# Second attention of a two-block kernel: probabilities divided before the transposes, values as the stationary operand, RMS factors applied to the two halves of the output projection

## The chip, the cores and the metric

The kernel runs on one core of a Trainium2 chip. The metric is the device time of one execution in microseconds (us), as the median over several executions.

## The reference

Two transformer blocks follow each other on 256 tokens of width 1024. The change lies in the second one. After its projections it has 8 query heads of kind A (windowed, two key/value heads, with one more "sink" score per head in the softmax denominator) and 8 heads of kind B (neighbourhood attention with a bias), all of width 64. Every query sees 256 latent keys and 256 context keys. Then each kind's 512 outputs are normalised by their own root mean square, and both go through one output projection:

```python
p = jax.nn.softmax(jnp.concatenate([s_loc, s_ctx, sink_col], axis=-1), axis=-1)      # kind A; kind B has no sink
o = einsum('bnkgqj,bnjkd->bnqkgd', p_loc, vb) + einsum('bnkgqj,bjkd->bnqkgd', p_ctx, v_ctx)
...
jnp.concatenate([_rms_norm(o_a, g_a), _rms_norm(o_b, g_b)], axis=-1) @ w_out
...
x = x + g1 * merged; x = x + g2 * swiglu(modulate(rms_norm(x)))
```

All is float32.

## The kernel before, in words

The program is one instruction stream per engine, written out by hand in its order; semaphores join them. The second attention works on 32 tiles (`tiles2`): token block b (128 queries) of 2, kind (0 is A, 1 is B), head h of 8. A tile has 128 queries by 512 keys. Tiles go in pairs p = 0 to 15: pairs 0 to 3 and 8 to 11 are kind A, the others kind B. "Pair A" and "pair B" below mean a pair of that kind.

- **TensorE.** For each p: `scores2(p)` (L985; 64-row products, the two tiles side by side in the array, and for the mask or bias full 128x128 ones), then `turn2` of both tiles of pair p-1 (L994; four 128x128 transposes each, of the exponentials E2), then `values2` of both tiles of pair p-2 (L1010; per tile four products with the transposed exponentials, 128x128, as the stationary operand and 64 columns of V moving). A float32 product is two records of the profile, a transpose one.
- **VectorE** takes each tile's row maximum (L2050 and, with the sink, L2051 for A; L2054 for B). After eight tiles it copies their outputs from PSUM (L2013, `outputs`); the division by the sums for eight heads of both kinds is done once per token block (L2025 to L2032, `divide`).
- **ScalarE** in iteration n takes the exponential of tile n (L1484, with the row sum as a second, small instruction) and then copies the transposed tile n-2 from PSUM (L1491). `sink_exp` (L1469) and the squares of the outputs (L1476) come once per token block.
- **Buffers.** E2 and PT2 (the transposed tiles) have four places each, the scores four PSUM banks, the transposes two, the outputs the two banks PSX.

Behind the loop TensorE transposes the normalised outputs of a block (`turn_block`, L1029), projects them (`project_out(b, half)`, L1037: eight products 128x128 by 128x512, one PSUM bank), turns the next block, and so on: turn 0, (0,0), turn 1, (0,1), (1,0), turn of the second norm's rows `hnx` 0, (1,1). VectorE adds each projected half to the residual (`add_attention`, L2076 and L2078), norms the rows (`normed_block`), and splits the columns and the first weights of the MLP into two float32r parts (L2102, L2103, `lower` L2096). Then TensorE starts the MLP (L1087). VectorE's order there is `add_attention(1,0)`, h3T of block 0, `split_columns(0)`, `lower(0)`, `add_attention(1,1)`, `normed_block(1)`, `lower(1)`. The inverse square roots are done by GpSimd (L2166).

```python
for p in range(NT // 2 + 2):
    if p < NT // 2:
        scores2(p)
    if 1 <= p <= NT // 2:
        turn2(2 * p - 2)
        turn2(2 * p - 1)
    if p >= 2:
        values2(2 * p - 4)
        values2(2 * p - 3)
```

## Time and profile before

| | |
|---|---|
| median of 3 runs | 921.19 us (920.28 to 921.21) |
| the profiled execution | 920.68 us |
| its span in the profile | 918.8 us |
| TensorE busy over the span | 837.0 us (91%) |
| VectorE, ScalarE, GpSimd busy | 393.3, 254.8, 56.5 us |
| chain that ended last, by engine | TensorE 77%, DMA 9%, VectorE 7% |
| second attention, first scores to last values | 611.95 to 690.43 us |
| first product of the MLP | 721.78 us |

The span is the part of an execution that the engines fill. A timeline row gives start and length in us, the engine (PE is TensorE's product, PEld its weight load, DVE VectorE, ACT ScalarE, POOL GpSimd), the line, what is written and read, and in brackets how long the engine had been idle before it and who released it. TensorE's products overlap, so the length of a group is a little more than the distance to the next one; the distance of starts is the cost in its queue. The granted clock is a share of 2.4 GHz.

### The profile page before, as it was taken

How to read it: one execution, taken by the hardware profiler on the slowest of the kernel's cores; microseconds unless marked ns; L12 is line 12 of the kernel's file. 1: busy time of each engine (PE TensorE's matmuls, PEld its weight loads, DVE VectorE, ACT ScalarE, POOL GpSimd, SP SyncE). 2: the span in 40 equal slices, each digit the busy share in tenths (PEclk: the TensorE clock that was granted, in tenths of full speed). 3: DMA queues.
4: the chain of work that ended last, by engine and by line, in shares of the span. 5: the costliest groups of instructions: out<-in, count | busy, mean ns of one | idle time of the engine just before them, and what ended most of it. 6: DMA issues, size and time to landing. Idle time of an engine off the chain costs nothing.

```text
span 918.8 us, 12887 instructions
## 1 busy us (share of the span) xinstructions
PE 837.0 (91%) x5247; PEld 585.2 (64%) x5247; DVE 393.3 (43%) x714; ACT 254.8 (28%) x410; POOL 56.5 (6%) x35
## 2 busy tenths in 40 slices
PE   9999999989968896887878589979999999999998
PEld 6866767766545563364255164458884688888886
DVE  1557154435270211011111255673434775665765
ACT  2242224421112121112112210025452343443431
POOL 1000032101030000000000001420000000000000
PEclk9989999989989999899799979989999999999999
DMA  9952446557496999999999993420000734644501
GB/s 327 310 195 92 168 165 218 200 213 275 156 348 248 403 405 404 409 404 405 409 405 405 406 330 139 163 91 1 1 1 0 274 138 139 236 175 161 206 1 46
DMA packets 124058, 208.40 MB, mean 227 GB/s; under 512 B 7625, under 2 KB 42730, under 8 KB 123890
## 3 DMA queue, kind: packets, MB, share of 16 engines
q1 hardware_dynamic: 121138, 203.52, 60.2%
q10 hardware_dynamic: 2816, 4.27, 1.5%
q8 instruction: 29, 0.48, 0.2%
q14 instruction: 11, 0.09, 0.0%
q0 software_dynamic: 64, 0.05, 0.0%
HBM read 206.74 MB, written 1.08 MB: 226 GB/s over the span
## 4 chain that ended last, share of the span: by engine, by line
PE 77%; DMA 9%; DVE 7%; issue 3%; ACT 1%; POOL 1%; SPq 0%; DVEq 0%; ACTq 0%; PEldq 0%; POOLq 0%
DMA arena<-in_w_down_dram 9%; PE psa L512 8%; PE psv L1087 4%; PE psa L1087 4%; PE psa L915 4%; PE psa L848 4%; PE psa L985 3%; PE psa L860 3%; PE psx L1010 3%; PE psv L872 3%; PE psa L747 2%; PE psx L899 2%; PE psv L1088 2%; PE psa L1088 2%; PE psx L539 2%
## 5 line engine op out<-in xcount | busy, mean ns | idle before, releaser
L2096 DVE TENSOR_TENSOR unit_parts<-ring,unit_parts 128x2048 fp32r<-128x2048 f32 x33 | 75.5, 2289 | 57.5 <-ACT unit_parts L1503 57.5
L1503 ACT ACTIVATE unit_parts<-ring 128x2048 fp32r<-128x2048 f32 x33 | 63.2, 1914 | 73.1 <-PE psa L1088 42.2
L512 PE MATMUL psa<-arena,ring 128*128 128x256 f32 x320 | 69.9, 380 | 1.0 <-ACT arena L1274 1.0
L1087 PE MATMUL psv<-column_parts,unit_parts 128*128 128x512 f32 (+1 forms) x192 | 65.5, 389 | 2.5 <-DVE arena L2123 1.4
L512 PEld LDWEIGHTS psa<-arena,ring 128*128 128x128 f32 x320 | 60.6, 190 | 10.3 <-DVE arena L1566 1.2
L915 PE MATMUL psa<-ring,arena 128*128 128x512 f32 (+1 forms) x160 | 64.3, 567 | 1.2 <-DVE arena L1568 1.2
L1087 PE MATMUL psa<-column_parts,unit_parts 128*128 128x512 f32 (+1 forms) x192 | 65.1, 387 | 0.0
L872 PE MATMUL psv<-ring,arena 128*32 128x256 f32 x1024 | 57.0, 380 | 0.0
L2166 POOL TENSOR_TENSOR small<-small,consts 128x2 f32<-128x2 f32 (+4 forms) x15 | 21.8, 1454 | 521.7 <-DVE small L1922 264.2
L915 PEld LDWEIGHTS psa<-ring,arena 128*128 128x128 f32 x160 | 31.9, 200 | 33.1 <-issue 30.1
L1088 PE MATMUL psv<-column_parts,unit_parts 128*128 128x256 f32 (+1 forms) x192 | 52.0, 271 | 0.0
L1088 PE MATMUL psa<-column_parts,unit_parts 128*128 128x256 f32 (+1 forms) x192 | 52.0, 271 | 0.0
L848 PE MATMUL psa<-arena 128*128 128x128 f32 x256 | 33.7, 296 | 16.2 <-DVE arena L1893 16.2
L848 PEld LDWEIGHTS psa<-arena 128*128 128x128 f32 x256 | 32.4, 209 | 22.2 <-issue 22.2
L872 PEld LDWEIGHTS psv<-ring,arena 128*32 128x32 f32 x1024 | 32.2, 110 | 21.9 <-DMA ring<-in_w_up_dram 1.0
L1910 DVE TENSOR_TENSOR residual<-residual,psx 128x512 f32<-128x512 f32 x16 | 11.0, 687 | 75.9 <-PE psx L899 75.9
L1087 PEld LDWEIGHTS psv<-column_parts,unit_parts 128*128 128x128 f32 x192 | 36.1, 188 | 10.3 <-DVE unit_parts L2096 2.9
L1087 PEld LDWEIGHTS psa<-column_parts,unit_parts 128*128 128x128 f32 x192 | 36.1, 188 | 7.5
L1088 PEld LDWEIGHTS psv<-column_parts,unit_parts 128*128 128x128 f32 x192 | 36.3, 189 | 0.6 <-issue 0.2
L1088 PEld LDWEIGHTS psa<-column_parts,unit_parts 128*128 128x128 f32 x192 | 36.4, 189 | 0.0
L889 PE MATMUL psx<-arena 128*32 128x512 f32 x128 | 22.4, 793 | 14.6 <-DMA arena<-in_w_down_dram 14.6
L1898 DVE COPY arena<-psa 128x256 f32 x8 | 3.4, 425 | 67.2 <-PE psa L860 67.2
(376 smaller groups left out, 1438.0 us busy)
## 6 DMA issues: line engine op xcount, KB each, us to landing
ring<-in_w_gate_dram SPq DMA_DIRECT2D x43, 1024.0 KB, 9.3
ring<-in_w_up_dram SPq DMA_DIRECT2D x43, 1024.0 KB, 5.2
arena<-in_w_down_dram SPq DMA_DIRECT2D x32, 1024.0 KB
ring<-in_w_in_dram SPq DMA_DIRECT2D x24, 1024.0 KB, 10.1
ring<-in_w_mod_dram SPq DMA_DIRECT2D x24, 1024.0 KB, 7.2
ring<-in_w_down_dram SPq DMA_DIRECT2D x11, 1024.0 KB, 7.3
ring<-in_w_out_dram SPq DMA_DIRECT2D x8, 1024.0 KB, 6.0
arena<-in_w_in_dram SPq DMA_DIRECT2D x8, 512.0 KB, 12.3
```

Source lines behind the costliest of these rows:

```text
L512: mm = pe.matmul(bank[:, cc * T:(cc + 1) * T], w, hT[:, k, :], start=(k == 0), stop=(k == KD - 1))
L848: mm = pe.matmul(mXT[half][:, kk * P:(kk + 1) * P], h2[:, b, k * P:(k + 1) * P], Pd[:, b, :, :].rearrange("p e s -> p (e s)"), start=(b == ...
L860: mm = pe.matmul(mXT[0][:, b * CTX_W:(b + 1) * CTX_W], hTc[:, k, b * P:(b + 1) * P], cw[:, k, :], start=(k == 0), stop=(k == KD - 1))
L872: mm = pe.matmul(mG[32 * e:32 * e + 32, f0:f0 + FF], XT[:, 2 * pair + kk, 32 * e:32 * e + 32], w[:, e, kk * FF:(kk + 1) * FF], start=(pair ...
L889: mm = pe.matmul(mY[half][32 * e:32 * e + 32, :], hidT[:, fc * P + 32 * e:fc * P + 32 * e + 32], w[:, e, :], start=(fc == 0), stop=(fc == 1))
L915: mm = pe.matmul(bank[:, 0:ncols], lhs[:, k, b * P:(b + 1) * P], units[k // per][:, k % per, :], start=(k == 0), stop=(k == KD - 1))
L985: mm = pe.matmul(o_, l_, r_, start=first, stop=last)
L1010: mm = pe.matmul(bank[:, h * HD:(h + 1) * HD], PT2[:, n % 4, m * P:(m + 1) * P], vs[m], start=(m == 0), stop=(m == 3))
L1087: pe.matmul(both_parts(bank, t_0, t_1), hi, col_parts[:, :, k, t_0:t_1], start=(k == 0), stop=False)
L1088: mm = pe.matmul(bank[:, t_0:t_1], lo, col_parts[:, 0, k, t_0:t_1], start=False, stop=(k == KD - 1))
L1503: act.activation(unit_parts[q % 3][:, 0, :], slot_of(NPRE + u_), ACT.Copy).then_inc(upper_done, 1)
L2096: vec.tensor_tensor(lo, slot_of(NPRE + at["mlp"] + 3 * n + kind), hi, ALU.subtract).then_inc(lower_done, 1)
```

## The change

1. **Division ahead of the transposes.** `norm_probs(n)` on VectorE adds the sink's term to the row sum (A only), takes the reciprocal and multiplies the 128x512 tile E2 by it in place. `turn2(n)` waits for it and no longer for the exponential. The sink's exponential is one 128x1 instruction per A tile on ScalarE, ahead of the tile's own.
2. **Values as weights.** `values2(p)` takes V (128x64) as the stationary operand and the transposed probabilities (128 columns) as the moving one; the two tiles of a pair write partitions 0 to 63 and 64 to 127. Outputs come transposed, features on the partitions. `PAIRS_A` pairs an even with an odd head. In TensorE's order it stands between the scores and the transposes.
3. **Outputs.** ScalarE squares a finished bank of eight tiles (`head_squares(k)`), and behind that VectorE writes it into oT with the gain (`outputs(k)`, four 128x128 instructions), in iterations n = 12, 20, 28 and 36 of both engines. No outputs are copied, divided, normed or transposed as rows any more.
4. **RMS factors.** The squares are summed by products with ones (`square_sums`, 128x128 by 128x2, four per token block and kind), behind the loop. The projection of each output half is kept as two sums, one per kind, in two banks. `add_attention` applies each kind's factor and the gate while reading its bank (one scalar_tensor_tensor) and adds it to the residual: four pairs of instructions per token block where there were two.
5. `turned_block(oT, ...)` and two of the `turn_block` calls go. oT and the squares have other places in SBUF.

```diff
-OUTPUTS_AT, SINK_AT, DIVIDE_AT, SQUARES_AT, NORM_AT = 19, 20, 22, 24, 26
+PAIRS_A = (0, 5, 1, 4, 2, 7, 3, 6)
+HEAD_POWERS = (12, 13)
...
-        sqo = ar(14336, 2, 512)
-        oT, h3T = ar(2048, KD, T), ar(0, KD, T)
+        sqo = ar(4096, 4, 4, P)
+        oT, h3T = ar(0, KD, T), ar(0, KD, T)
-        onat = ar(4096, NB, D)
...
-                  for h in ((0, 4, 1, 5, 2, 6, 3, 7) if kind == 0 else range(8))]
+                  for h in (PAIRS_A if kind == 0 else range(8))]
...
             def turn2(n):
-                pe.wait_ge(exps2_done, n + 1)
+                pe.wait_ge(probs2_normed, n + 1)
                 if n >= 2:
                     pe.wait_ge(probs2_copied, n - 1)
                 for m in range(4):
                     mm = pe.transpose(TB[n % 2][:, m * P:(m + 1) * P], E2[:, n % 4, m * P:(m + 1) * P], ident)
                 mm.then_inc(turned2_done, 1)
-            def values2(n):
-                pe.wait_ge(probs2_copied, n + 1)
...
+            def values2(p):
+                steps = []
+                for n in (2 * p, 2 * p + 1):
+                    pe.wait_ge(probs2_copied, n + 1)
+                    b, kind, h = tiles2[n]
+                    if n % 8 == 0 and n >= 16:
+                        pe.wait_ge(values2_copied, n // 8 - 1)
+                    r0, c0 = HD * (h % 2), P * (h // 2)
+                    if kind == 0:
+                        vs = [pA[:, m, 640 + HD * (h // 4):640 + HD * (h // 4) + HD] for m in range(2)]
+                        vs += [cA[:, m, 128 + HD * (h // 4):128 + HD * (h // 4) + HD] for m in range(2)]
+                    else:
+                        vs = [pB[:, m, 1024 + h * HD:1024 + (h + 1) * HD] for m in range(2)]
+                        vs += [cB[:, m, 512 + h * HD:512 + (h + 1) * HD] for m in range(2)]
+                    steps.append([(PSX[n // 8 % 2][r0:r0 + HD, c0:c0 + P], vs[m], PT2[:, n % 4, m * P:(m + 1) * P])
+                                  for m in range(4)])
+                for m, two in enumerate(zip(*steps)):
+                    for o_, l_, r_ in two:
+                        mm = pe.matmul(o_, l_, r_, start=(m == 0), stop=(m == 3))
+                        if m == 3:
+                            mm.then_inc(values2_done, 1)
             for p in range(NT // 2 + 2):
                 if p < NT // 2:
                     scores2(p)
+                if p >= 2:
+                    values2(p - 2)
                 if 1 <= p <= NT // 2:
                     turn2(2 * p - 2)
                     turn2(2 * p - 1)
-                if p >= 2:
-                    values2(2 * p - 4)
-                    values2(2 * p - 3)
...
+            halves = {(0, 0): (PSV[(nv + 2) % 3], PSA[(na + 2) % 3]), (0, 1): (PSV[nv % 3], PSA[na % 3]),
+                      (1, 0): (PSV[(nv + 1) % 3], PSA[(na + 1) % 3]), (1, 1): (PSX[0], PSX[1])}
+            at["halves"] = halves
+            def square_sums(k):
+                pe.wait_ge(heads_squared, k + 1)
+                for cc in range(4):
+                    mm = pe.matmul(PSX[0][:, 2 * k:2 * k + 2], sqo[:, k, cc, :], c("ones")[:, 0:2],
+                                   start=(cc == 0), stop=(cc == 3))
+                mm.then_inc(sums2_ready, 1)
             def project_out(b, half):
-                bank = v_bank()
-                for k in range(KD):
...
+                for kind in range(2):
+                    for k in range(4 * kind, 4 * kind + 4):
+                        mm = pe.matmul(halves[b, half][kind][:], oT[:, k, b * P:(b + 1) * P],
+                                       out_units[2 * half + k // 4][:, k % 4, :], start=(k % 4 == 0), stop=(k % 4 == 3))
+                    mm.then_inc(halves_ready, 1)
+            pe.wait_ge(values2_copied, 3)
+            for k in range(3):
+                square_sums(k)
+            project_out(0, 0)
+            project_out(0, 1)
+            pe.wait_ge(power_req, HEAD_POWERS[0])
+            square_sums(3)
+            pe.wait_ge(values2_copied, 4)
+            project_out(1, 0)
+            freed2.extend([(halves_ready, 6)] * 2)
             pe.wait_ge(rows_normed, 5)
-            turn_block(onat, 0)
-            pe.wait_ge(v_free, nv)
...
             turn_block(hnx, 0)
             h0_at = nv
             at["h", 0] = na
+            pe.wait_ge(power_req, HEAD_POWERS[1])
             project_out(1, 1)
-            freed2.extend([(v_ready, nv)] * 2)
+            freed2.extend([(halves_ready, 8)] * 2)
             pe.wait_ge(v_free, h0_at)
             pe.wait_ge(a_free, na)
-            pe.wait_ge(values2_copied, 4)
...
-            def sink_exp(b):
-                act.wait_ge(sink_req, b + 1)
...
+            def head_squares(k):
+                act.wait_ge(values2_done, 8 * (k + 1))
+                act.activation(sqo[:, k, :, :], PSX[k % 2][:].rearrange("p (c t) -> p c t", c=4),
+                               ACT.Square).then_inc(heads_squared, 1)
+            for n in range(NT + 5):
                 if n < NT:
                     act.wait_ge(max2_done, n + 1)
+                    b, kind, h = tiles2[n]
+                    if kind == 0:
+                        act.activation(den[:, stat(n):stat(n) + 1], sink[:, h:h + 1], ACT.Exp,
+                                       bias=nm2[:, stat(n):stat(n) + 1]).then_inc(sink_exp_done, 1)
                     if n >= 4:
                         act.wait_ge(turned2_done, n - 3)
                     act.activation(E2[:, n % 4, :], SB[n % 4][:], ACT.Exp, bias=nm2[:, stat(n):stat(n) + 1],
                                    accum_out=rs2[:, stat(n):stat(n) + 1]).then_inc(exps2_done, 1)
-                if n >= 2:
+                if 2 <= n < NT + 2:
                     m = n - 2
                     act.wait_ge(turned2_done, m + 1)
                     if m >= 4:
                         act.wait_ge(values2_done, m - 3)
                     act.activation(PT2[:, m % 4, :], TB[m % 2][:], ACT.Copy).then_inc(probs2_copied, 1)
-                if n == SINK_AT:
-                    sink_exp(0)
-                if n == SQUARES_AT:
-                    head_squares(0)
+                if n % 8 == 4 and n > 8:
+                    head_squares(n // 8 - 1)
...
-            sink_exp(1)
-            turned_block(oT, 0, vc[:, ROWS["on_a"]:ROWS["on_a"] + KD])
-            head_squares(1)
-            turned_block(oT, 1, vc[:, ROWS["on_a"]:ROWS["on_a"] + KD])
             act.wait_ge(values2_done, NT)
-            act.wait_ge(heads_squared, 2 * NB)
             upper(0)
             for b in range(NB):
-                act.wait_ge(attention_added, b + 1)
+                act.wait_ge(halves_added, 4 * b + 4)
                 act.activation(hnx[:, b, :], xres[:, b, :], ACT.Square, accum_out=ss[:, b:b + 1]).then_inc(squares_done, 1)
...
+            def norm_probs(n):
+                b, kind, h = tiles2[n]
+                j = stat(n)
+                dve.wait_ge(exps2_done, n + 1)
+                total = rs2[:, j:j + 1]
+                if kind == 0:
+                    link(vec.tensor_tensor(total, total, den[:, j:j + 1], ALU.add))
+                link(vec.reciprocal(total, total))
+                vec.tensor_scalar(E2[:, n % 4, :], E2[:, n % 4, :], total, None, ALU.mult).then_inc(probs2_normed, 1)
             def outputs(k):
-                dve.wait_ge(values2_done, 8 * (k + 1))
-                vec.tensor_copy(onat[:, k // 2, 512 * (k % 2):512 * (k % 2) + 512], PSX[k % 2][:]).then_inc(values2_copied, 1)
...
+                b, kind = divmod(k, 2)
+                dve.wait_ge(heads_squared, k + 1)
+                for cc in range(4):
+                    row = ROWS["on_a"] + 4 * kind + cc
+                    ins = vec.tensor_scalar(oT[:, 4 * kind + cc, b * P:(b + 1) * P], PSX[k % 2][:, cc * P:(cc + 1) * P],
+                                            vc[:, row:row + 1], None, ALU.mult)
+                ins.then_inc(values2_copied, 1)
             def head_norm(b):
-                dve.wait_ge(heads_squared, 2 * (b + 1))
-                rsqrt(ss5[:, 2 * b:2 * b + 2], rs5[:, 2 * b:2 * b + 2], 512)
...
+                nonlocal nrs
+                dve.wait_ge(sums2_ready, 3 + b)
+                nrs += 1
+                assert nrs == HEAD_POWERS[b]
+                vec.tensor_scalar(rs5[:, 2 * b:2 * b + 2], PSX[0][:, 4 * b:4 * b + 4].rearrange("p (k c) -> p k c", c=2)[:, :, 0],
+                                  1.0 / 512, EPS, ALU.mult, ALU.add).then_inc(power_req, 1)
+            for n in range(NT + 5):
                 if n < NT:
                     b, kind, h = tiles2[n]
                     j = stat(n)
...
                                           ALU.max, ALU.mult).then_inc(max2_done, 1)
                     else:
                         vec.tensor_reduce(nm2[:, j:j + 1], src, AX, ALU.max, negate=True).then_inc(max2_done, 1)
-                if n % 8 == 3 and n > 8:
+                if 1 <= n <= NT:
+                    norm_probs(n - 1)
+                if n % 8 == 4 and n > 8:
                     outputs(n // 8 - 1)
-                if n == OUTPUTS_AT:
-                    dve.wait_ge(max2_done, 16)
...
+            head_norm(0)
             def add_attention(b, half):
-                bank = v_take()
                 xv = xres[:, b, half * 512:half * 512 + 512]
-                tm = (t0, t1)[half]
-                if b > 0:
...
+                gate = gbc[:, 0, half * 512:half * 512 + 512]
+                for kind in range(2):
+                    m = 4 * b + 2 * half + kind
+                    dve.wait_ge(halves_ready, m + 1)
+                    if m % 4 == 0:
+                        dve.wait_ge(power_done, HEAD_POWERS[b])
+                    if m >= 2:
+                        dve.wait_ge(halves_added, m - 1)
+                    tm = (t0, t1)[kind]
+                    link(vec.scalar_tensor_tensor(tm, at["halves"][b, half][kind][:], rs5[:, 2 * b + kind:2 * b + kind + 1], gate,
+                                                  ALU.mult, ALU.mult))
+                    if m > 0:
+                        dve.wait_ge(halves_added, m)
+                    vec.tensor_tensor(xv, xv, tm, ALU.add).then_inc(halves_added, 1)
...
             add_attention(0, 0)
-            turned_block(oT, 1, vc[:, ROWS["on_a"]:ROWS["on_a"] + KD])
             add_attention(0, 1)
+            head_norm(1)
             normed_block(0)
```

The first place is TensorE's queue in the loop, for one pair B whose values are the first of a bank used before. Before (L985 scores, L994 transposes, L1010 values):

```order
L985 MATMUL psa<-arena,consts 128x256 x2
L985 MATMUL psa<-arena 128x256 x2
L994 MATMUL psv<-consts,arena 128x128 [waits probs2_copied,exps2_done]
L994 MATMUL psv<-consts,arena 128x128 x3
L1010 MATMUL psx<-arena 128x64 [waits values2_copied,probs2_copied]
L1010 MATMUL psx<-arena 128x64 x3
L1010 MATMUL psx<-arena 128x64 [waits probs2_copied]
```

And now (L986, L1017, L995):

```order
L986 MATMUL psa<-arena,consts 128x256 x2
L986 MATMUL psa<-arena 128x256 x2
L1017 MATMUL psx<-arena 64x128 [waits probs2_copied,values2_copied]
L1017 MATMUL psx<-arena 64x128 x7
L995 MATMUL psv<-consts,arena 128x128 [waits probs2_copied,probs2_normed]
L995 MATMUL psv<-consts,arena 128x128 x3
```

The values moved ahead of the transposes, the eight products of a pair have one shape of 64x128, and the transposes wait for `probs2_normed`.

The second place is VectorE's queue around n = 12, where the first bank of outputs is written (L2052 maximum, L2020 and L2021 `norm_probs`, L2029 `outputs`). Now:

```order
L2052 TENSOR_REDUCE small<-psa 128x1 [waits scores2_done]
L2020 RECIPROCAL small<-small 128x1 [waits exps2_done]
L2021 TENSOR_SCALAR arena<-arena,small 128x512 [waits dve_chain]
L2029 TENSOR_SCALAR arena<-psx,vec_cols 128x128 [waits heads_squared]
L2029 TENSOR_SCALAR arena<-psx,vec_cols 128x128 x3
L2052 TENSOR_REDUCE small<-psa 128x1 [waits scores2_done]
```

Before, at n = 11:

```order
L2054 TENSOR_REDUCE small<-psa 128x1 [waits scores2_done] x3
L2054 TENSOR_REDUCE small<-psv 128x1 [waits scores2_done]
L2013 COPY arena<-psx 128x512 [waits values2_done]
L2054 TENSOR_REDUCE small<-psa 128x1 [waits scores2_done] x3
L2054 TENSOR_REDUCE small<-psv 128x1 [waits scores2_done]
```

The maximum of tile 13 now stands behind four instructions that wait for ScalarE's squares; before, one copy stood there that waited for TensorE's values.

## Rows read from the trace of the kernel before

**Rows 1.** Windows view, 18.7 us of pairs: span, busy (instructions) per engine, clock, DMA share, GB/s
```profile
628.00:646.70 18.70, 18.70 (x138) 14.78 (x136) 5.84 (x9) 9.01 (x23) 0.00 (x0) 1.00 0.00 1
```
**Rows 2.** Timeline, weight loads around one pair A: start us, us, engine, line, tiles
```profile
656.23 0.52 PEld L985 LDWEIGHTS psa<-arena 64*128 64x128 f32 x8
...
658.15 0.86 PEld L994 LDWEIGHTS psv<-consts,arena 128*128 128x128 f32 x8 [0.33 <-issue]
658.98 1.86 PEld L1010 LDWEIGHTS psx<-arena 128*128 128x128 f32 x16
660.91 0.18 PEld L985 LDWEIGHTS psa<-arena 64*128 64x128 f32 x1
```
**Rows 3.** Timeline, the same around one pair B
```profile
665.59 0.30 PEld L985 LDWEIGHTS psa<-arena 64*128 64x128 f32 x4
...
667.91 0.86 PEld L994 LDWEIGHTS psv<-consts,arena 128*128 128x128 f32 x8 [0.33 <-issue]
...
670.67 0.18 PEld L985 LDWEIGHTS psa<-arena 64*128 64x128 f32 x1
```
**Rows 4.** Timeline, VectorE's maxima of a pair A, and of a pair B
```profile
658.25 0.69 DVE L2050 TENSOR_REDUCE small<-psa 128x1 f32<-128x512 f32 x1 [1.15 <-PE psa L985]
658.98 0.21 DVE L2051 TENSOR_SCALAR small<-small,sinks 128x1 f32<-128x1 f32 x1
...
668.01 1.29 DVE L2054 TENSOR_REDUCE small<-psa 128x1 f32<-128x512 f32 x2 [1.40 <-PE psa L985]
```
**Rows 5.** Timeline, ScalarE behind the first of those maxima
```profile
659.23 0.69 ACT L1484 ACTIVATE arena<-psa,small 128x512 f32<-128x512 f32 x1 [2.25 <-DVE small L2051]
659.82 0.19 ACT L1484 ACTIVATION_READ_ACCUMULATOR arena<-psa,small 128x1 f32 x1
659.91 0.59 ACT L1491 ACTIVATE arena<-psv 128x512 f32<-128x512 f32 x1
660.39 0.21 ACT L1469 ACTIVATE small<-small 128x8 f32<-128x8 f32 x1
```
**Rows 6.** Groups of lines: xcount, busy us, mean ns, idle before
```profile
L1719 DVE RECIPROCAL small<-small 128x2 f32<-128x2 f32 x8 | 1.3, 165 | 8.4 <-ACT arena L1364 8.4
```
**Rows 7.** Timeline, VectorE: scalings of two 128x512 tiles in SBUF, of four 128x128 from PSUM
```profile
691.42 1.12 DVE L2005 TENSOR_SCALAR arena<-psv,vec_cols 128x128 f32<-128x128 f32 x4
...
696.27 0.88 DVE L2040 TENSOR_SCALAR arena<-arena,small 128x512 f32<-128x512 f32 x2 [0.81 <-POOL small L2166]
```
**Rows 8.** Timeline, the first two tiles' transposes
```profile
615.77 0.42 PEld L994 LDWEIGHTS psv<-consts,arena 128*128 128x128 f32 x4 [0.52 <-ACT arena L1484]
...
616.62 0.42 PEld L994 LDWEIGHTS psv<-consts,arena 128*128 128x128 f32 x4 [0.43 <-ACT arena L1484]
```
**Rows 9.** Timeline, column tiles: loads of a 128*64 alone, products of 128*32 four abreast
```profile
147.78 0.25 PEld L680 LDWEIGHTS psx<-arena 128*64 128x64 f32 x2
...
468.59 2.80 PE L872 MATMUL psv<-ring,arena 128*32 128x256 f32 x48
```
**Rows 10.** Timeline, TensorE from the last scores to the MLP
```profile
680.83 0.18 PEld L985 LDWEIGHTS psa<-arena 64*128 64x128 f32 x1
...
690.43 0.48 PEld L1029 LDWEIGHTS psv<-consts,arena 128*128 128x128 f32 x4
...
700.69 13.90 PE L1037 MATMUL psv<-ring,arena 128*128 128x512 f32 x32
...
721.78 0.67 PE L1087 MATMUL psv<-column_parts,unit_parts 128*128 128x256 f32 x1
```
**Rows 11.** Timeline, the seam to the MLP: VectorE's last attention sum, TensorE's wait for its norm
```profile
719.35 2.28 DVE L2096 TENSOR_TENSOR unit_parts<-ring,unit_parts 128x2048 fp32r<-128x2048 f32 x1
...
722.37 0.69 DVE L2076 TENSOR_TENSOR arena<-psv,arena 128x512 f32<-128x512 f32 x1 [0.74 <-PE psv L1037]
...
726.64 0.66 PE L1029 MATMUL psv<-consts,arena 128*128 128x128 f32 x4 [0.66 <-DVE arena L2089]
```

**Rows 12.** Windows view as in rows 1, a stretch in which TensorE waits
```profile
603.00:605.00 2.00, 0.00 (x0) 0.00 (x0) 1.93 (x4) 0.00 (x0) 0.00 (x0) 0.69 1.07 380
```

86 lines of the change are left out of this document (4 added, 82 removed).

## The prediction

> **What bounds the kernel now.** I read the windows view first. In a stretch of pairs TensorE is busy for the whole time at the full clock, VectorE for a third and ScalarE for a half of it [rows 1]. The reader should look at the last two as spare time, but only as a sum: the change puts VectorE between the exponential and the transposes, so order counts and not load. The timeline then gives the pairs. A pair A lasts 4.68 us (656.23 to 660.91): scores 1.92, transposes 0.83, values 1.93 [rows 2]. A pair B lasts 5.08 (665.59 to 670.67), with scores of 2.32 [rows 3]. The values are 16 weight loads of 128 columns in 1.86 us, one each 0.111 us, and 0.17 us on top before the scores, which use the array in another shape [rows 2]. Other engines only answer: VectorE starts 0.10 us behind the scores' end (658.15 to 658.25), and idled before that [rows 2, 4].
>
> **TensorE's saving in the loop.** With V as weights, two tiles use different columns of the array. The nearest rows are column tiles of 32 columns, four abreast: 48 records of 256 moving columns took 2.80 us, 12 rounds of 0.21 and a tail, so they do run together, and loads of 64 columns follow each other by 0.11 us in one tile [rows 9]. I take 8 rounds of 0.111 us and one change of shape, 0.17: 1.06 us for a pair's values. The transposes now also end in a change of shape, 0.17. Left to TensorE, a pair A would last 1.92 + 1.06 + 0.83 + 0.17 = 3.98 and a pair B 4.38. The bounds for the values are 0.95 and, if the two tiles take turns, 1.94 (as now).
>
> **What comes between.** VectorE now does, in this order: maximum of tile 2p, division of tile 2p-1, maximum of 2p+1, division of 2p. The second tile's transposes so wait for a division that is queued behind a maximum that itself waits for the new scores. Durations: a maximum A is 0.73 to its small instruction plus 0.13 (0.21 less the 0.08 by which neighbours overlap); a maximum B 0.60, two of 0.69 lying in 1.29 [rows 4]. A reciprocal is 0.165 and I take 0.20 with the 0.04 that a dependent start costs [rows 4, 6], and 0.20 for adding the sink. The scaling of 128x512 in SBUF is 0.48 and holds the queue 0.40, two of them in 0.88 [rows 7]; 0.05 for the signal, as between ScalarE's last small instruction and the transposes. Counted from the end of the scores:
>
> Pair A: 0.10 + 0.86 + 0.20 + 0.20 + 0.48 + 0.05 = 1.89. TensorE is there at 1.06 + 0.41 = 1.47 and waits 0.42. Then 0.41 + 0.17 + 1.92: the pair lasts 4.39, 0.29 less than now.
>
> Pair B: 0.10 + 0.60 + 0.20 + 0.48 + 0.05 = 1.43, hidden behind 1.47. The pair lasts 4.38, 0.70 less. Where A turns to B the first division is still one of A (4.54, 0.54 less, twice), where B turns to A 0.49 less, once.
>
> From the third scores to the last there are 13 intervals: five A (-1.45), five B (-3.50), two A to B (-1.08), one B to A (-0.49): -6.5 us.
>
> **The start.** There is no earlier pair to hide behind. The first transposes (615.77) come later by the sink's exponential, 0.10 (a row of this kind is 0.21 long [rows 5] and neighbours on that queue overlap), and by 0.93 of division. The second (616.62) follow the first division (0.80 of queue), the maximum of tile 2 (0.86) and their own division (0.93) from 615.87, so 618.46 [rows 8]: +1.84 us.
>
> **The outputs.** In iteration 12 VectorE's `outputs(0)` waits for ScalarE's square, which is queued behind the copy of tile 10, which waits for its transposes; and the maximum of tile 13 is queued behind `outputs(0)`. Pair B, from the scores' end: transposes of tile 10 readable at 1.06 + 0.71 = 1.77; copy 0.48 [rows 5]: 2.25; square, as long as the copy, with its signal 0.68: 2.93; four scalings from PSUM, 1.12 for four, holding the queue 1.04 [rows 7]: 3.97; maximum 13: 4.70; exponential 13, 0.59 and 0.09: 5.38; copy of tile 11, with signal 0.65: 6.03. TensorE wants tile 11 for `values2` at 4.37: it stands 1.66 us. In iteration 20, a pair A, the same chain gives 6.47 against 4.39, but the following wait of 0.42 is then gone: 1.66 again. Two such stalls lie inside the 13 intervals: +3.3, which leaves -3.2.
>
> **The end of the loop.** Now it is 9.60 us from the last scores' start to the last values' end (680.83 to 690.43) [rows 10]. After: the third stall, iteration 28, lets values 26 and 27 start at 3.98. Transposes of 28 and 29 from 5.04; copy of 28, exponential 31, copy of 29: 7.56; values, 1.06; transposes 30 and 31, two copies: 10.46; values: 11.52. +1.9 us. The loop's sum is +1.84 - 3.2 + 1.9 = +0.6.
>
> **Behind the loop.** TensorE now needs 31.35 us from 690.43 to 721.78: four projections of 16 records at 0.43 (13.90 for two), three turns of 0.87, a wait of 1.5 [rows 10]. After: four projections, one turn of `hnx`, and `square_sums`, 32 loads at 0.111, 3.55 us, in the queue ahead of and between the projections; the wait goes, because `oT` of block 0 is long written. 27.5 + 0.87 + 3.55 = 31.9 against 31.6 by the same addition: +0.3. The factors are computed during the projections, and `normed_block(0)` has 7.8 us of projection and sums as cover. At the seam VectorE's `lower(0)` ends at 721.63; `add_attention(1,1)` was then two instructions from 722.37, done at 723.8; now it is four of 0.72 from 721.63, done at 724.5. Behind it come the norm for which TensorE stands already (0.66 idle, then `lower(1)`) [rows 11]. +0.7.
>
> **Sum.** +0.6 + 0.3 + 0.7 = +1.6. The profiled execution was 920.68, so 922.2; the median of the runs lies 0.5 above it, so 922.7. Queue positions and DMAs: the second block's weights are freed by the same projections as before, and nothing moves on SyncE; GpSimd's two small powers stay hidden. So a shorter TensorE queue buys no time: what it gives up comes back as waits for VectorE and ScalarE.
>
> **The rivals.** A difference under 0.2% (1.8 us) is what a measurement of this kernel can't tell from none. The forecast's own range is 920.5 to 925, from steps of VectorE shorter by 0.05 us (1 us in all) and values of 0.95 to 1.2 us per pair.
>
> *The two column tiles take turns* (7 in 100). A pair's values then cost 1.94 and stand ahead of the transposes: pairs A 4.85 and B 5.26, 0.17 longer than now, 13 times, 2.2; no saving of 6.5; the rest as above. About 934. For it: no row has 64-column tiles abreast. Against it: the four of 32 [rows 9]. The Trainium skill ("TensorE: Matmul & The Clock Gate", Part 3, "The mechanism") says that a weight load overlaps running products only where its row group differs. Both tiles use all row groups, so by that rule loads would stand between the products and this case would come. The trace disagrees: loads in one row group lie beside their products at 0.11 us each [rows 9].
>
> *Column tiles overlap in part* (8 in 100): values of 1.3 to 1.5 us, 925 to 928, since above 1.06 each tenth lies on the path of the B pairs.
>
> *The clock falls* (9 in 100). Where TensorE stood for several us, the granted clock went to 0.69 in the mean, that is to the lower of 1.2 and 2.4 GHz for a part [rows 12]. The new stalls are 1.7 us and follow each other closely at the loop's end (1.7, 1.5, 0.9), with nearly empty products of two columns behind. If half of the first projection's 6.9 us of work ran at 1.2 GHz, 3.4 us come on top: 926.
>
> *TensorE stays the bound* (8 in 100), the case on the fast side. If ScalarE and VectorE ran ahead enough, pairs of 3.98 and 4.38 without stalls: 13 times -0.7 is -9.1; with +1.8, +1.0, and nothing at the outputs, about -6: 915. It decides where the division is readable before 1.47 us; for A it is 0.4 short, so this asks for steps a fifth shorter than their rows.
>
> **How the numbers follow.** The forecast has 68 in 100: of it some 4 fall under 919.4, 39 within 0.2% of 921.19, 25 above 923.0. With the rivals: faster 0.12, same 0.40, slower 0.48. The range of 919.0 to 928.0 leaves out the first and last rival and little else.
>
> **What would show it.** Right: `values2` records in pairs with near-equal starts and 1.06 us per pair; B pairs of 4.4 and A pairs of 4.4 with TensorE idle 0.4 before the second transposes, released by L2021; three idles of TensorE before L1017 of about 1.7 us; the last values 0.6 us later relative to the first scores; the MLP's first product 0.3 later still, and 0.7 at the seam. Wrong: A pairs near 4.0 (VectorE not in the way), L1017 groups of 1.9 (no overlap), a clock under 1.00 between 611 and 740, or no idle before L1017.

## The result and the profile after

| | before | after |
|---|---|---|
| median of the runs | 920.74 us (4 runs, 919.88 to 921.21) | 928.69 us (4 runs, 927.24 to 929.28) |
| ratio | 1 | 1.0085, 95% interval 1.0068 to 1.0103 |
| span of the profiled execution | 918.8 us | 926.6 us |
| granted TensorE clock, mean | 0.960 | 0.954 |

The changed kernel is 7.9 us slower. The forecast was 922.7 with a range up to 928.0: the direction was among the likely ones, the size was not. Three parts of the span can be cut out of either profile in the same way: from the first scores to TensorE's last record with the values ("loop"), from there to the MLP's first product ("projections"), and from there to the end ("rest"). The end of the loop is taken at the start of the record that follows the last values. The place where the attention hands over to the MLP, inside the rest, is called the seam.

One execution of e5 below (978.39 us, mean granted clock 0.833) and one of the kernel before beside each group of runs were slow: the ratios leave them out, and e5's median of 917.38 would be 917.25 without its one.

| part | before | after | difference | forecast |
|---|---|---|---|---|
| start to first scores | 611.95 | 611.74 | -0.2 | 0 |
| loop | 78.59 | 80.77 | +2.2 | +0.6 |
| projections | 31.24 | 33.32 | +2.1 | +0.3 |
| rest | 197.02 | 200.77 | +3.8 | +0.7 |

Each part is longer than forecast by 1.6 to 3.1 us. The windows view of the changed kernel, over the same program as before and with the columns of [rows 1], says what all three have in common (span, busy times of PE, PEld, DVE, ACT and POOL, then the granted clock):

```profile
660.00:664.00 4.00, 1.92 (x16) 1.27 (x16) 3.36 (x11) 1.91 (x5) 0.00 (x0) 1.00 0.00 0
664.00:670.00 6.00, 5.90 (x36) 4.04 (x36) 2.35 (x9) 2.89 (x8) 0.00 (x0) 0.72 0.00 0
670.00:680.00 10.00, 10.00 (x91) 6.87 (x89) 5.91 (x16) 5.32 (x13) 0.00 (x0) 1.00 0.01 2
692.40:695.20 2.80, 2.80 (x28) 2.69 (x25) 1.12 (x4) 2.40 (x2) 0.00 (x0) 1.00 0.02 6
695.20:700.40 5.20, 5.20 (x10) 2.19 (x10) 0.16 (x1) 0.00 (x0) 0.71 (x1) 0.67 0.00 0
700.40:710.00 9.60, 9.60 (x24) 4.31 (x23) 4.33 (x6) 0.00 (x0) 0.00 (x0) 1.00 0.00 0
...
733.40:739.00 5.60, 5.54 (x26) 5.54 (x27) 5.40 (x7) 2.29 (x3) 0.00 (x0) 0.50 1.04 385
739.00:745.00 6.00, 6.00 (x49) 6.00 (x49) 0.00 (x0) 0.79 (x1) 0.00 (x0) 0.91 0.04 11
```

Three times the clock goes from the 2.4 to the 1.2 GHz level and comes back: at 665.0, at 695.8 and at 733.3 (the falls "at 664", "in the first projection" and "at the seam" in what follows). The kernel before shows 1.00 in the same places:

```profile
664.00:670.00 6.00, 6.00 (x46) 4.89 (x46) 3.80 (x8) 3.70 (x10) 0.00 (x0) 1.00 0.01 3
...
692.80:699.80 7.00, 6.92 (x16) 3.10 (x17) 2.61 (x7) 1.33 (x4) 0.70 (x1) 1.00 0.00 1
...
728.80:734.00 5.20, 5.16 (x45) 5.16 (x45) 5.13 (x7) 2.28 (x3) 0.00 (x0) 1.00 1.06 403
```

The timeline of TensorE in the changed kernel around these places (start us, us, engine, line, tiles, count, and in brackets the idle time ahead with its releaser) shows what came before each fall:

```profile
657.46 1.09 PE L1017 MATMUL psx<-arena 128*64 128x128 f32 x16
...
659.34 0.66 PE L995 MATMUL psv<-consts,arena 128*128 128x128 f32 x4 [0.20 <-DVE arena L2021]
...
664.10 1.13 PE L1017 MATMUL psx<-arena 128*64 128x128 f32 x16 [2.18 <-ACT arena L1500]
...
684.93 1.09 PE L1017 MATMUL psx<-arena 128*64 128x128 f32 x16 [1.56 <-ACT arena L1500]
...
688.54 1.09 PE L1017 MATMUL psx<-arena 128*64 128x128 f32 x16 [1.50 <-ACT arena L1500]
...
691.49 1.09 PE L1017 MATMUL psx<-arena 128*64 128x128 f32 x16 [0.83 <-ACT arena L1500]
692.51 2.84 PE L1048 MATMUL psx<-consts,arena 128*128 128x2 f32 x24
695.21 5.38 PE L1056 MATMUL psv<-ring,arena 128*128 128x512 f32 x8
700.42 3.60 PE L1056 MATMUL psa<-ring,arena 128*128 128x512 f32 x8
...
731.26 0.66 PE L1035 MATMUL psv<-consts,arena 128*128 128x128 f32 x4 [1.22 <-DVE arena L2082]
...
733.46 0.58 PE L1102 MATMUL psv<-column_parts,unit_parts 128*128 128x256 f32 x1 [1.11 <-DVE unit_parts L2089]
```

What the reader should see: the values' group L1017 is 1.02 to the next record, where [rows 2] had 1.93, so TensorE's saving is there. But the third and the fourth row show TensorE standing for ScalarE's copy, 2.18 and 1.56 us; another of 1.56 ends at 644.91, so there is one such stall for each of the first three banks of outputs. Then the projection's first eight records take 5.21 us to the start of the next eight (695.21 to 700.42), and those 3.44. Without its fall that group costs 1.8 us less. In the loop, 6.00 us at a mean of 0.72 is 1.7 us lost, if all the work there goes by the clock. The seam's fall covers 5.6 us at 0.50 and a part of the next 6; a run below, in which it is absent, puts it at 3.0. Together 6.5 of the 7.8 us.

### The profile page after: what moved, and what is told of

Same layout as the page of the kernel before. It is cut to its first block, busy times and chain, and to the rows that moved or that the text cites. A ratio compares the mean times of both kernels' runs of the same rounds, so it can differ in the third digit from the quotient of the medians.

```text
span 926.6 us, 12999 instructions
## 1 busy us (share of the span) xinstructions
PE 835.4 (90%) x5263; PEld 576.3 (62%) x5263; DVE 413.6 (45%) x790; ACT 255.9 (28%) x412; POOL 56.5 (6%) x35
## 4 chain that ended last, share of the span: by engine, by line
PE 75%; DMA 9%; DVE 9%; issue 3%; ACT 2%; POOL 1%; SPq 0%; DVEq 0%; ACTq 0%; PEldq 0%; POOLq 0%
DMA arena<-in_w_down_dram 9%; PE psa L513 8%; PE psv L1102 5%; PE psa L1102 4%; PE psa L916 4%; PE psa L849 4%; PE psa L861 3%; PE psv L873 3%; PE psa L986 3%; PE psa L748 2%; PE psx L900 2%; PE psv L1103 2%; PE psa L1103 2%; PE psx L540 2%; PE psv L523 2%
## 5 line engine op out<-in xcount | busy, mean ns | idle before, releaser
L1102 PEld LDWEIGHTS psv<-column_parts,unit_parts 128*128 128x128 f32 x192 | 37.2, 194 | 10.4 <-DVE unit_parts L2089 2.8
L1102 PEld LDWEIGHTS psa<-column_parts,unit_parts 128*128 128x128 f32 x192 | 37.2, 194 | 7.6
L1103 PEld LDWEIGHTS psv<-column_parts,unit_parts 128*128 128x128 f32 x192 | 37.5, 195 | 0.6 <-issue 0.2
L1103 PEld LDWEIGHTS psa<-column_parts,unit_parts 128*128 128x128 f32 x192 | 37.4, 195 | 0.0
```

Source lines behind the costliest of these rows:

```text
L1102: pe.matmul(both_parts(bank, t_0, t_1), hi, col_parts[:, :, k, t_0:t_1], start=(k == 0), stop=False)
L1103: mm = pe.matmul(bank[:, t_0:t_1], lo, col_parts[:, 0, k, t_0:t_1], start=False, stop=(k == KD - 1))
```

## The experiments

All profiled spans are read in the same three parts, since the place of the first scores alone, in front of all that was edited, varied from 609.7 to 612.4. "Falls" lists the places behind 614 us where a window of two microseconds has a clock under 0.99. Ratios are to executions of the kernel before taken alongside (medians 920.38 beside e1 to e4, 920.08 beside e5 to e8, 920.51 beside e9 to e12), with their 95% interval; they are not the quotient of the medians in the table.

| run | median us (ratio, interval) | loop | projections | rest | falls |
|---|---|---|---|---|---|
| before | 920.74 | 78.59 | 31.24 | 197.02 | none |
| after | 928.69 (1.0085, 1.0068 to 1.0103) | 80.77 | 33.32 | 200.77 | loop, projection, seam |
| e1 | 920.52 (1.0005, 0.9995 to 1.0016) | 74.13 | 33.32 | 200.75 | projection, seam |
| e2 | 922.86 (1.0030, 1.0018 to 1.0043) | 80.75 | 31.62 | 197.81 | loop |
| e3 | 923.89 (1.0046, 1.0028 to 1.0064) | 80.77 | 33.31 | 197.75 | loop, projection |
| e4 | 917.59 (0.9980, 0.9967 to 0.9992) | 73.13 | 33.31 | 199.34 | projection, seam |
| e5 | 917.38 (0.9957, 0.9938 to 0.9977) | 74.16 | 31.62 | 197.78 | none |
| e6 | 914.07 (0.9935, 0.9915 to 0.9954) | 77.53 | 24.75 | 197.55 | none |
| e7 | 932.57 (one run) | 84.85 | 34.99 | 199.32 | projection, seam |
| e8 | 927.33 (one run) | 78.59 | 38.26 | 197.13 | projection |
| e9 | 923.31 (1.0026, 1.0005 to 1.0047) | 78.60 | 33.96 | 197.21 | none |
| e10 | 915.74 (0.9960, 0.9944 to 0.9976) | 74.14 | 31.62 | 197.80 | none |
| e11 | 919.95 (0.9995, 0.9977 to 1.0013) | 74.15 | 33.32 | 200.48 | projection, seam |
| e12 | 914.23 (0.9944, 0.9927 to 0.9961) | 73.12 | 31.62 | 197.72 | none |

**e1: the outputs one iteration later.** My theory was that the stalls come from a queue position and the falls of the clock from the stalls; this takes the stalls in the loop away. VectorE reads the finished bank behind the maximum that it held up.

```diff
-            for n in range(NT + 5):
+            for n in range(NT + 6):
...
-                if n % 8 == 4 and n > 8:
+                if n % 8 == 5 and n > 8:
                     outputs(n // 8 - 1)
```

> The changed kernel with one thing moved: VectorE writes a finished bank of outputs in iterations 13, 21, 29 and 37 instead of 12, 20, 28 and 36, so that the maximum of tile 13 (21, 29) is no longer queued behind it; ScalarE's squares stay where they are. No work is added or removed. Theory (the stalls of TensorE before the values come from that queue position, and the falls of the granted clock come from the stalls): the three idles of 1.6, 2.2 and 1.6 us before the values of tiles 10, 18 and 26 go, 5.0 us by the same addition as in the prediction, and the fall of the clock behind the second of them (0.67 and 0.76 from 664 to 670, 1.9 us) goes with them: 928.7 - 6.9 = 921.8; should the idles at the loop's end be what makes the clock fall at 695, that one stays. Rival (the clock falls for another reason, such as the new shape 128*64 of the values or the products with two moving columns, and would fall here too): 928.7 - 5.0 = 923.7, with a clock under 1.00 still somewhere between 650 and 690. If the stalls have another cause than the queue position: no change, 928.7.

The loop is 6.6 us shorter (80.77 to 74.13). The three stalls were 1.56, 2.18 and 1.56, 5.3 us; the fall at 664, 1.7 us, went with them, and a wait of 0.44 ahead of transposes, which the second stall had covered, came back: 6.6. Here is the place in the timeline of this run; no idle stands before L1017:

```profile
658.67 1.09 PE L1017 MATMUL psx<-arena 128*64 128x128 f32 x16
659.69 1.41 PE L995 MATMUL psv<-consts,arena 128*128 128x128 f32 x8
663.35 1.09 PE L1017 MATMUL psx<-arena 128*64 128x128 f32 x16
```

So by the medians one statement moved by an iteration pays for the whole loss, within what can be measured (1.0005, 0.9995 to 1.0016). The three parts of the two traces add up to 308.20 here and to 306.85 before, so 1.4 us of the loss are still there; the rest of the 8.2 between the medians lies ahead of the first scores (611.74 and 610.10), where nothing was edited. The other two falls stay, unchanged in size.

**e2: 128 columns of ones in the square sums.** The 24 records with two moving columns follow each other by 0.11 us, as weight loads of 128 columns do [rows 2], so 128 moving columns should cost next to nothing more.

```diff
-                    mm = pe.matmul(PSX[0][:, 2 * k:2 * k + 2], sqo[:, k, cc, :], c("ones")[:, 0:2],
+                    mm = pe.matmul(PSX[0][:, k * P:(k + 1) * P], sqo[:, k, cc, :], c("ones"),
...
```

My theory fell for this place. The waits ahead of the sums are as in the changed kernel, and the projection runs at full clock: its part is 31.62 instead of 33.32, and the group of 24 records costs 0.08 more (2.78 to the next, 2.70 with two columns). The seam's fall is gone too, which neither theory had.

**e3: a dummy product in each wait of the seam**, one 128x128 by 128x512 into a free bank, ahead of the transposes of `h3T` and ahead of the second `lower`. Its result is not read.

```diff
+                            pe.wait_ge(halves_added, 8)
+                            for _ in range(1):
+                                pe.matmul(PSX[0][:], ident, c("window"), start=True, stop=True)
                             pe.wait_ge(rows_normed, 6)
                             turn_block(hnx, 1)
+                            for _ in range(1):
+                                pe.matmul(PSX[0][:], ident, c("window"), start=True, stop=True)
```

> The changed kernel with two products more, 128x128 by 128x512, into a free PSUM bank whose result nobody reads: one while TensorE waits 1.22 us for the second norm's rows, one while it waits 1.11 us for the second weights of the MLP. Each is two records of 0.43 us, shorter than the wait. Theory (the clock falls at about 733 because of these two waits, one close behind the other): the clock stays at 1.00 from 725 to 745, the products of the MLP's first unit come 0.12 and not 0.21 us apart, and the 2.9 to 3.3 us that the fall costs come back: 925.6. Rival (the fall has nothing to do with the waits): the same fall, 928.7 to 929.2.

```profile
727.90 1.07 PE L1126 MATMUL psx<-consts 128*128 128x512 f32 x2
729.28 0.66 PE L1035 MATMUL psv<-consts,arena 128*128 128x128 f32 x4 [0.31 <-DVE arena L2087]
729.77 0.60 PE L1035 MATMUL psa<-consts,arena 128*128 128x128 f32 x4
730.21 1.02 PE L1130 MATMUL psx<-consts 128*128 128x512 f32 x2
```

The waits shrink from 1.22 to 0.31 and from 1.11 to 0.24, the seam keeps its clock, and the rest is 197.75 where the changed kernel has 200.77: that fall costs 3.0 us, and useless work of 2 us that delays nothing buys it back. What is left, 197.75 less 197.02, is the term of the seam that I had summed, 0.7.

**e4: maxima in pairs, then divisions in pairs**, with ScalarE's squares at n % 8 == 3 and the outputs at 5.

```diff
-                if 1 <= n <= NT:
+                if n % 2 == 1 and n < NT:
                     norm_probs(n - 1)
+                    norm_probs(n)
...
```

> The changed kernel with VectorE's order in the loop turned: maximum 2p, maximum 2p+1, division 2p, division 2p+1, so that no division waits behind a maximum that waits for new scores; squares in iterations 11, 19, 27, 35 and outputs in 13, 21, 29, 37. Theory (order and not load holds the loop): pairs A of 4.0 and B of 4.4 us, the loop ends 6.4 us earlier than before the change and not 2.4 later, 928.7 - 8.8 = 919.9; with a fall of the clock at the loop's end and one at the seam still in it. If VectorE's load were the limit, pairs A would stay at 4.4 and it would come out as the run with the outputs late.

The loop is 73.13, 1.0 less than with e1, and TensorE's second wait of each pair A is gone. The loop ends 5.5 us earlier than before the change and not the 6.4 that was expected; two new waits for ScalarE's copy stand in it (1.18 and 0.69). The median is 2.3 better than expected, but the profiled execution took 920.00, the slowest of the ten, so its trace can't say where the 2.3 lie. In it the rest is 199.34 against 200.75 in e1, because the seam's fall is half as long: it lasts from 727.1 to 730.5, in e1 from 724.8 to 731.7.

**e5: the edits of e1 and e2 together.** The question is whether each fall has its own cause.

> The changed kernel (928.7) with two edits at once: VectorE's scalings of the outputs one iteration later (alone: 920.5) and 128 columns of ones moved in the square sums (alone: 922.9). Theory A, each clock fall has a cause of its own near its place: the fall of the first projection goes with the wide ones and is worth 1.8 us, the seam's fall stays, about 918.7. Theory B, the wide sums also keep the clock up at the seam, as the profile of that run alone showed: 1.8 and some 2.5 more, about 916. Theory C, the two edits removed the same thing (at the loop's first stall and behind it): 920.5.

No fall is left behind the first scores, though the waits at the seam are still 1.22 and 1.11 and those at the loop's end 1.50 and 0.83. That is theory B; its number was 916, the median is 917.4. Each part is what the part's own edit gave alone.

**e6: all edits together**, and block 0's first projection moved into the loop's last two iterations, where TensorE waited.

```diff
+                if p >= NT // 2:
+                    kind = p - NT // 2
...
+                    project_half(0, 0, kind)
...
-            project_out(0, 0)
```

> The changed kernel with maxima and divisions in pairs and outputs late (alone: 917.6), 128 columns of ones in the square sums, one dummy product in each of the two waits of the seam, and block 0's first output projection moved into the last two iterations of the loop, in front of the last two products with the values, where TensorE idled 1.5 and 0.8 us (the dummy product's result is not read). Theory, the edits add up: 917.6 - 1.8 (no fall in the first projection) - 2.3 (the two idles filled) - 2.5 (no fall at the seam) = 911.0; 909.5 to 913 with what new orders cost. Rival, the waits only move to VectorE's and ScalarE's copies behind the moved halves and clock falls come elsewhere: 915 to 917.

**e12: the edits of e4 and e2 without the moved projection and the dummies**, as in the two diffs above.

> The changed kernel with maxima and divisions in pairs and outputs late (alone: 917.6) and 128 columns of ones, without dummy products and with all projections behind the loop. The run with these and with the moved projection and the dummies took 914.1, not the 911.0 that the sum gave. Theory, the edits before add up (-1.8 in the first projection, -2.5 at the seam): 913.3, and the moved projection brought nothing. Rival, the moved projection brought its 2.3 us and the clock gives less here: 915 to 916.5.

The sum had given 911.0 for e6, up to 913; 914.07 misses it. In the profiles, loop and projections together are 102.28 in e6 and 104.74 in e12; the waits of 1.50 and 0.83 are in e12 alone, so the move brought 2.5 there. The medians are 914.07 and 914.23, so it does not show there; the intervals of the ratios leave room for it. The profiled execution of e6 took 911.54 at a mean clock of 0.964, its other three 913.85 to 914.38 at 0.960 to 0.962. A mean lower by 0.003 over 910 us would be 2.7 us lost (an estimate), so a lower clock may be what hides the gain; that isn't shown, as those three left no trace. For e12 the theory said 913.3 and its rival 915 or more: the median lies between, nearer to the theory. Both kernels beat the changed one and the one before, by about 14.5 and 6 us. The timeline of e12 at the loop's end and at the first projection:

```profile
679.09 1.09 PE L1017 MATMUL psx<-arena 128*64 128x128 f32 x16 [1.50 <-ACT arena L1500]
680.12 1.09 PE L995 MATMUL psv<-consts,arena 128*128 128x128 f32 x8
682.04 1.09 PE L1017 MATMUL psx<-arena 128*64 128x128 f32 x16 [0.83 <-ACT arena L1500]
683.06 2.94 PE L1048 MATMUL psx<-consts,arena 128*128 128x128 f32 x24
```

**e7: the two column tiles one after the other** instead of product by product.

```diff
-                for m, two in enumerate(zip(*steps)):
-                    for o_, l_, r_ in two:
+                for one in steps:
+                    for m, (o_, l_, r_) in enumerate(one):
```

> The changed kernel with the pair's eight products of the values issued tile by tile (four into columns 0 to 63, then four into columns 64 to 127), not in alternation. Theory, the two column tiles run side by side only because their records alternate: here a pair's group takes 1.9 us in place of 1.02 to 1.09, so some 0.85 more on the pairs that TensorE bounds; of 16 pairs three stand in a stall, so 11 to 12 us: 936 to 941. Rival, a load of 64 columns costs 0.06 us in any order: the group stays under 1.3 us and the time within 3 us of 928.7.

```profile
L1017 PE MATMUL psx<-arena 128*64 128x128 f32 x256 | 25.2, 278 | 7.8 <-ACT arena L1500 7.8
```

The same row of the changed kernel, from the view of groups by line (busy us, mean ns, idle before):

```profile
L1017 PE MATMUL psx<-arena 128*64 128x128 f32 x256 | 17.5, 278 | 7.6 <-ACT arena L1500 7.6
```

25.2 us over 16 groups is 1.58 each, against 1.09: both expectations miss. The alternation is worth 0.49 us per pair. To the next record a group takes 1.51 here, 1.02 in the changed kernel and 1.93 before, so about half of the saving is there without it. The loop is 4.1 us longer in spite of having no fall at 664; that its stall in iteration 20, 2.40, is longer than the 2.18 of the changed kernel and yet brings no fall shows that the length of a wait does not decide by itself.

**e8 and e9: dummy square sums in the kernel before**, 12 products of 128x128 weights ahead of the first turn; e8 moves 2 columns, e9 128. This kernel has no stalls in its loop. The results are not read.

```diff
+            pe.wait_ge(values2_copied, 3)
+            for _ in range(12):
+                pe.matmul(PSX[0][:, 0:2], c("window")[:, 0:P], c("ones")[:, 0:2], start=True, stop=True)
```

(e9 has `[:, 0:P]` in both places of `[:, 0:2]`.)

> The kernel before (920.7) with 12 dummy products of 128x128 weights by two moving columns (24 records, the square sums' shape; their result is not read) behind the loop, ahead of the first turn of block 0. Their own time is 2.8 us. Theory, such products count for the clock like idle TensorE: the granted clock falls below 0.8 in the stretch behind them and the first projection's products go from 3.4 to over 4.5 us, about 925 to 926. Rival, it takes the stalls of the changed kernel before them too, and the clock stays up: 923.4.

> The kernel before (920.7) with the same 12 dummy products behind the loop as in the run with two moving columns, but of 128 moving columns (their result is not read). The two-column ones made the clock fall to 0.50 and took 6.7 us of span, 2.8 of them their own time. Theory, it is the number of moving columns that the clock reacts to, not the weight loads and not the place: no fall, 2.9 us of their own, 923.5. Rival, any group there makes the fall (the idle of 1.3 us before the first projection comes behind it): 927.

Two columns, timeline:

```profile
690.11 3.35 PE L1044 MATMUL psx<-consts 128*128 128x2 f32 x24
693.32 1.09 PE L1029 MATMUL psv<-consts,arena 128*128 128x128 f32 x4
694.21 1.06 PE L1029 MATMUL psa<-consts,arena 128*128 128x128 f32 x4
696.55 10.01 PE L1037 MATMUL psv<-ring,arena 128*128 128x512 f32 x16 [1.28 <-DVE arena L2008]
```

128 columns, the same instructions:

```profile
690.83 2.90 PE L1044 MATMUL psx<-consts 128*128 128x128 f32 x24
693.56 0.60 PE L1029 MATMUL psv<-consts,arena 128*128 128x128 f32 x4
694.00 0.60 PE L1029 MATMUL psa<-consts,arena 128*128 128x128 f32 x4
695.88 7.10 PE L1037 MATMUL psv<-ring,arena 128*128 128x512 f32 x16 [1.28 <-DVE arena L2008]
```

This is the plainest pair of the study. The wait of 1.28 is the same, the records are as many, and the group of dummies costs 2.73 with 128 columns. With two, the mean clock over the group itself is already 0.82 (windows view, 690.1 to 693.3), so it falls ahead of the wait; behind the group it is 0.50 and 0.55 up to 703, and the part of the projections is 4.3 us longer (38.26 against 33.96). The one execution of e8 is 4.0 above the median of e9, the two profiled ones differ by 3.5.

**e10 and e11: two columns in some of the sums only**, from e5: in the fourth alone (8 records, between the third and the fourth projection), or in the first three alone (24 records).

```diff
-                    mm = pe.matmul(PSX[0][:, k * P:(k + 1) * P], sqo[:, k, cc, :], c("ones"),
+                    mm = pe.matmul(PSX[0][:, k * P:k * P + (2 if k == 3 else P)], sqo[:, k, cc, :], c("ones")[:, 0:(2 if k == 3 else P)],
```

(e11 has `k < 3` in place of `k == 3`.)

> The kernel with outputs late and 128 columns of ones (917.4, no fall anywhere from 612 to 760 in its profile), with two columns again in the fourth square sum alone, 8 records of 0.95 us between the third and the fourth projection, 15 us ahead of the seam. Theory, the fall at the seam comes from its own waits and from what was nearly empty shortly before: the fall comes back at the seam only, 2.5 us more, 920. Rival, only the group of 24 records behind the loop counts: no fall, 917.4.

> The same kernel (917.4) with two columns in the first three square sums (24 records behind the loop) and 128 in the fourth. Theory as for the run with the fourth alone: a fall in the first projection only, 1.8 us, 919.2, and the seam at full clock. Rival, once the clock has fallen in the first projection the seam's waits bring it down again, so both falls come: 920.5 to 922.

The eight records do nothing. That e10's median is 1.6 below e5's has no counterpart in the traces, whose three parts agree within 0.02, nor in the ratios (0.9960 and 0.9957). The 24 bring both falls back, the one behind them and that at the seam, 38 us later. Windows of e11:

```profile
688.30:693.50 5.20, 5.20 (x10) 2.20 (x10) 0.16 (x1) 0.00 (x0) 0.71 (x1) 0.67 0.00 0
693.50:703.80 10.30, 10.30 (x25) 4.56 (x24) 4.33 (x6) 0.00 (x0) 0.00 (x0) 1.00 0.00 0
...
726.50:733.00 6.50, 6.45 (x31) 6.46 (x31) 5.39 (x7) 2.29 (x3) 0.00 (x0) 0.50 0.91 337
```

Windows of e10, the same work:

```profile
687.50:690.90 3.40, 3.40 (x11) 1.49 (x10) 0.16 (x1) 0.00 (x0) 0.71 (x1) 1.00 0.00 0
...
723.90:730.00 6.10, 6.07 (x53) 6.07 (x53) 5.38 (x7) 2.27 (x3) 0.00 (x0) 1.00 0.96 355
```

The rival of e11 is right in kind, with 919.95 where it said 920.5 to 922. Of its ten executions the two fastest, 915.67 and 917.54, have a mean clock of 0.966 and 0.964, and the two slowest, 921.28 and 922.26, 0.955. That suggests that the falls come in most executions and not in all, but it isn't shown: the kernel before, which has no fall behind 614 in its trace, has executions from 916.41 at 0.967 to 921.68 at 0.957 as well.

## Why the prediction was wrong

**The step that failed is the clock.** The sum held it at full speed from the first scores to the MLP, and "the clock falls" was a rival of 9 in 100 with one place, the first projection, and one price, 3.4 us for half of it at 1.2 GHz. There were three places: 1.7 in the loop, 1.8 in the first projection, 3.0 at the seam. Its condition was wrong as well: for that place it named the new stalls as the cause and the products of two columns as something beside them. e2 kept the stalls and lost the fall; e8 has two-column products without the stalls and has the fall. Stalls are the cause in the loop (e1) and at the seam (e3), which the rival did not name. The rows of before [rows 12] had shown a wait as the only thing that lowers the clock. The rows of before hold no group like L1048, so the price of its effect on the clock had no bound there, and I should have said that and given the range room for it.

**The other terms were right to about 0.5 us.**

- *The loop*, +0.6: measured +2.2, of which 1.7 is the fall (3.4 us at 0.50). Pairs and start are as forecast: transposes at 616.66 and 618.30 (forecast, from 615.77 + 1.03, 616.80, and 618.46; the first scores stand 0.21 earlier than before), the wait before the second transposes 0.44 on the load side (0.42), released by L2021, and a pair A of 4.39 (653.07 to 657.46 between the value groups in the trace).
- *The stalls at the outputs*, three of 1.66: the trace has 1.56, 2.18 and 1.56. The one of 2.18, in iteration 20, is no miss: the forecast had 6.47 against 4.39 there, 2.08 of standing, and took off the wait of 0.42 that then goes. Its chain is the forecast's: the square L1481 behind a copy, `outputs` behind the square, the maximum behind `outputs`. ScalarE and VectorE in the changed kernel:

```profile
659.40 0.58 ACT L1500 ACTIVATE arena<-psv 128x512 f32<-128x512 f32 x1
659.87 0.59 ACT L1481 ACTIVATE arena<-psx 128x512 f32<-128x512 f32 x1
...
662.51 0.29 ACT L1489 ACTIVATE small<-sinks,small 128x1 f32<-128x1 f32 x1 [2.04 <-DVE small L2049]
```

```profile
660.50 1.12 DVE L2029 TENSOR_SCALAR arena<-psx,vec_cols 128x128 f32<-128x128 f32 x4 [1.22 <-ACT arena L1481]
661.54 0.68 DVE L2048 TENSOR_REDUCE small<-psa 128x1 f32<-128x512 f32 x1
```

  VectorE idles 1.22 for the square, and ScalarE then 2.04 for the maximum that stands behind `outputs` in VectorE's queue. e1 confirms it: without this order the loop is 4.5 us shorter than in the kernel before. The forecast's own numbers give the same, 0.6 less three stalls of 1.66, -4.4.
- *The values as column tiles*, 1.06 us per pair: measured 1.02 to the next record. By the rule of the Trainium skill ("TensorE: Matmul & The Clock Gate", Part 3, "The mechanism") loads would overlap products only in another row group. The trace disagrees: here all records use all row groups, and 16 loads and products take 1.02 us together. e7 adds that in one column tile at a time they take 1.51. The rival built on it said 934, which its terms don't give: 922.7 + 6.5 + 2.2 is 931.4.
- *Behind the loop*, +0.3: the part of the projections is 31.62 without a fall, 0.08 of it for the wider sums, 31.24 before. *The seam*, +0.7: 197.72 to 197.81 without a fall (197.55 in e6), 197.02 before.

With the full clock the changed kernel would thus have taken 928.7 - 6.5 = 922.2, within 0.5 of the 922.7 of the forecast. The 6.5 us of the three falls stand where the sum had put nothing. The 922.2 is worked out, not measured: no run of the changed kernel keeps the stalls of its loop without their fall.

**What stays open.** Why one of three stalls in the loop (2.18) brings a fall and the longer one of e7 does not. And why the seam, with the same waits in e5 and in e11, keeps its clock only if the clock had not fallen in the first projection. TensorE at the seam of e5:

```profile
723.54 0.66 PE L1035 MATMUL psv<-consts,arena 128*128 128x128 f32 x4 [1.22 <-DVE arena L2082]
...
725.74 0.39 PE L1102 MATMUL psv<-column_parts,unit_parts 128*128 128x256 f32 x1 [1.11 <-DVE unit_parts L2089]
```

And of e11:

```profile
724.35 0.66 PE L1035 MATMUL psv<-consts,arena 128*128 128x128 f32 x4 [1.22 <-DVE arena L2082]
...
726.55 0.58 PE L1102 MATMUL psv<-column_parts,unit_parts 128*128 128x256 f32 x1 [1.10 <-DVE unit_parts L2089]
```

The chip's look at TensorE may lie differently in time against the program once 1.8 us have been lost; the Trainium skill ("TensorE: Matmul & The Clock Gate", Part 1, "What's actually happening") says that it is not aligned to the kernel and that the point of transition moves from run to run. The traces agree in that the 24 to 32 changes of the granted clock in each of the fourteen stand on one even grid, to 0.002 us, whatever the program does there; call its points marks. They don't show the spread: a mark stands 1.3 to 1.6 us ahead of the first scores in all fourteen. In e5 a mark at 723.6 lies between the two idles. In e11 none does, and the clock falls at the mark of 726.1, 0.45 us before the second idle ends. It is so in all nine traces with these waits: a mark stands between the idles, or within 0.1 us of that, in e2, e5, e10 and e12, and the larger part of both lies between two neighbouring marks in the changed kernel, e1, e4, e7 and e11, which are the five with the fall. The loop goes the same way: the stall of 2.18 lies whole between two marks, and a mark cuts the 2.40 of e7 into 0.6 and 1.8. So position alone accounts for what was left open, and a fall in the first projection would act by moving the program 1.8 us against the marks. This is worked out from the traces, and no run moved the seam by itself to test it; for the seams, though not for e7's loop, a memory of the earlier fall would account as well. Position is not what parts e8 from e9, or e5 from e11: the next mark comes 2.1 and 1.9 us behind the start of the 24 records in the first pair, 3.0 in both of the second.

## What to carry to other kernels

A product that takes as long as its weight load can move more columns at next to no cost in its own time (0.08 us in 24 records); a group of nearly empty ones, 2.7 us long itself, cost 1.8 to 4.3 us more through the clock here. Where a step hands data between two other engines, put it behind the instruction for which the bound engine waits: `outputs` one iteration later was worth 6.6 us in the loop, as much as the 6.5 that the rearranged products save in the sum. And cut the span into parts and read the granted clock of each before explaining a difference by instructions.
